# Retention in a hybrid decoder step: new tokens' outputs in four quarters of the array, scores in four banks, earlier copies of turned tokens

## The reference, cut to what matters

```
def retention_chunk(q, k, v, s_prev, log_gamma):
    scores = jnp.einsum('bihd,bjhd->bhij', qf, kf) * decay[None]
    o_intra = jnp.einsum('bhij,bjhe->bihe', scores, vf)
    q_decay = jnp.exp((idx + 1.0)[:, None] * log_gamma[None, :])
    o_inter = jnp.einsum('bihd,bhde->bihe', qf, s_prev) * q_decay[None, :, :, None]
    s_new = jnp.exp(C * log_gamma)[None, :, None, None] * s_prev + jnp.einsum('bjhd,hj,bjhe->bhde', kf, k_decay, vf)
    return o_intra + o_inter, s_new
```

## Time and profile before

| | |
|---|---|
| runs | 1435.70, 1435.81, 1437.54 us; median 1435.81 |
| profiled execution | 1436.48 us, of which the profile's span is 1434.7 us |
| busy in the span | PE 1374.4 us (96%), DVE 766.0 (53%), ACT 610.1 (43%), POOL 311.4 (22%) |
| mean granted clock of PE | 0.983 of full speed |

### The profile page before, as it was taken

The page is one execution under the profiler, slowest core; times in us unless marked ns, Lnnn a source line. Parts: engine busy times, 40 slices in busy tenths (PEclk is TensorE's granted clock), DMA queues, the critical chain, the costliest instruction groups (busy, mean ns, idle before and its releaser), DMA issues.

```text
span 1434.7 us, 31573 instructions
## 1 busy us (share of the span) xinstructions
PE 1374.4 (96%) x11123; PEld 1307.5 (91%) x11123; DVE 766.0 (53%) x1448; ACT 610.1 (43%) x1496; POOL 311.4 (22%) x487
## 2 busy tenths in 40 slices
PE   7984999999999999999989999999999999999998
PEld 7863888899999999999989888899999999999998
DVE  7772444536575575575554666455564443344443
ACT  3641333356565565565543444432233322233211
POOL 6530000046454555455410000000130000000000
PEclk9986999999999999999999999999999999999999
DMA  5123222166564565565545444332232222222232
GB/s 202 50 59 96 68 68 68 68 180 182 154 184 139 171 180 147 168 188 157 157 153 208 167 137 138 120 128 88 96 102 88 89 103 88 88 88 100 84 110 88
DMA packets 109325, 177.59 MB, mean 124 GB/s; under 512 B 13073, under 2 KB 84050, under 8 KB 107346
## 3 DMA queue, kind: packets, MB, share of 16 engines
q1 hardware_dynamic: 109202, 176.05, 38.4%
HBM read 163.98 MB, written 11.89 MB: 123 GB/s over the span
## 4 chain that ended last, share of the span: by engine, by line
PE 80%; DMA 4%; ACT 2%; DVE 2%; issue 2%; SPq 2%; POOL 0%; ACTq 0%; DVEq 0%; POOLq 0%
PE ps L1664 33%; PE ps L1376 24%; PE ps L1828 6%; PE ps L651 6%; PE ps L1402 2%; DMA z<-z_scratch 2%; PE ps L714 1%; PE ps L732 1%; PE ps L1882 1%; PE ps L1392 1%; DMA ring_raw<-in_wmain 1%; DMA ring_raw<-in_reto 1%; PE ps L724 1%; PE ps L1871 1%; SPq L983 0%
## 5 line engine op out<-in xcount | busy, mean ns | idle before, releaser
L1376 PE MATMUL ps<-wq_hi,ct_hi 128*128 128x260 f32 x1024 | 301.4, 294 | 1.4 <-POOL ct_lo L1052 1.4
L1376 PE MATMUL ps<-wq_hi,ct_lo 128*128 128x260 f32 x1024 | 289.5, 283 | 0.0
L1376 PE MATMUL ps<-wq_lo,ct_hi 128*128 128x260 f32 x1024 | 289.3, 283 | 0.0
L1052 POOL TENSOR_TENSOR ct_lo<-ct_raw,ct_hi 128x256 fp32r<-128x256 f32 x256 | 189.2, 739 | 390.4 <-ACT ct_hi L1111 196.8
L1220 DVE TENSOR_REDUCE k_sums<-k_squares 128x8 f32<-128x512 f32 (+1 forms) x256 | 175.3, 685 | 173.7 <-ACT k_squares L1118 171.4
L1118 ACT ACTIVATE k_squares<-ps 128x512 f32<-128x512 f32 x256 | 153.3, 599 | 164.4 <-PE ps L1376 160.3
L1376 PEld LDWEIGHTS ps<-wq_hi,ct_hi 128*128 128x128 f32 x1024 | 193.2, 189 | 4.9 <-issue 3.8
L1376 PEld LDWEIGHTS ps<-wq_lo,ct_hi 128*128 128x128 f32 x1024 | 193.1, 189 | 0.0
L1376 PEld LDWEIGHTS ps<-wq_hi,ct_lo 128*128 128x128 f32 x1024 | 192.6, 188 | 0.0
L1559 ACT ACTIVATE ring_hi<-ring_raw 128x1024 fp32r<-128x1024 f32 x88 | 89.1, 1013 | 167.6 <-PE ps L1664 120.4
L1564 DVE TENSOR_TENSOR ring_lo<-ring_raw,ring_hi 128x1024 fp32r<-128x1024 f32 x88 | 110.6, 1257 | 27.0 <-ACT ring_hi L1559 25.6
(11 more groups left out here) (324 smaller groups left out, 2967.1 us busy)
## 6 DMA issues: line engine op xcount, KB each, us to landing
ct_raw<-in_ct SPq DMA_DIRECT2D x256, 144.0 KB, 2.2
c_values<-in_c SPq DMA_DIRECT2D x256, 128.0 KB, 2.4
ring_raw<-in_wmain SPq DMA_DIRECT2D x40, 512.0 KB, 3.6
ring_raw<-in_up SPq DMA_DIRECT2D x32, 512.0 KB, 3.2
ring_raw<-in_down SPq DMA_DIRECT2D x32, 512.0 KB, 3.3
z_scratch<-z_staged SPq DMA_DIRECT2D x16, 268.0 KB, 2.2
z<-z_scratch SPq DMA_DIRECT2D x4, 1072.0 KB, 5.3
state_new<-in_state SPq DMA_DIRECT2D x4, 1024.0 KB, 4.8
```

Source lines behind the costliest of these rows:

```text
L1052: nc.gpsimd.tensor_tensor(ctl[:, j, :], ct[:, half, j, 0:KVL], cth[:, j, :].bitcast(F32), ALU.subtract).then_inc(ct_lo, 1)
L1376: mm = nc.tensor.matmul(k_ps[j % 2][:, f, 0:WQN], ch[:, j, r * P:(r + 1) * P], of_sequence(w, b)[:, r, f, :], start=(r == 0 and x == 0), s ...
```

## The change

- `new_outputs`: the masked queries get 32 columns each (24 of them zero), and product b goes to quarter b mod 4 of the array: rows 32 (b mod 4) and up of one PSUM bank. ACT copies the four partial tiles out together (`take_quarters`, r = 9), and at r = 10 PE adds them with one product with a constant 0/1 matrix (`sum_quarters`). Taking tile 5 out moves from r = 9 to r = 10.
- `scores`: tiles 2 and 3 go to the two banks of `ps[0]`, tile 4 to the first bank of `ps[1]`.
- ACT copies tiles 1, 3 and 5 of the turned tokens at the start of slots r = 3, 4, 5, ahead of the split.
- DVE runs `max_of_heads` in slot 2.
- The first mixing product waits for result tile k when it comes to it, not for all eight.

```
-                if slot == 3:
+                if slot == 2:
                     max_of_heads(b)
...
+    def score_place(self, t):
+        return self.ps[(1, 1, 0, 0, 1)[t]][:, t % 2, :]
...
             elif h:
                 pe.wait_ge(self.tok_out, self.copies * h)
+                pe.wait_ge(self.s_done, NT * h - 1)
+                pe.wait_ge(self.sm_done, NT * h - 1)
...
-            if t >= 2:
-                pe.wait_ge(self.sm_done, NT * h + t - 1)
-                pe.wait_ge(self.s_done, NT * h + t - 1)
+            if t in (2, 3):
+
+                pe.wait_ge(self.tok_out, self.copies * h + (2 * NT if t == 2 else self.copies))
+            if t == 4:
+                pe.wait_ge(self.sm_done, NT * h + 1)
+                pe.wait_ge(self.s_done, NT * h + 1)
...
             for b in range(NB):
-                mm = nc.tensor.matmul(ps[2][0:NB, NT % 2, 0:DV], self.qm[:, b, :], self.sd[:, b, :], start=(b == 0), stop=(b == NB - 1))
-            mm.then_inc(self.o_done, 1)
+                at = 32 * (b % 4)
+                mm = nc.tensor.matmul(ps[2][at:at + 32, NT % 2, 0:DV], self.qm[:, b, :], self.sd[:, b, :], start=(b < 4), stop=(b >= 4),
+                                      skip_group_check=True)
+            mm.then_inc(self.quad_done, 1)
+
+        def sum_quarters(h):
+            pe.wait_ge(self.quad_out, h + 1)
+            nc.tensor.matmul(ps[2][0:NB, NT % 2, 0:DV], m.const("sel"), self.quads[:], start=True, stop=True).then_inc(self.o_done, 1)
...
+                if r == 10:
+                    sum_quarters(h)
...
+        def take_quarters(h):
+            act.wait_ge(self.quad_done, h + 1)
+            nc.scalar.activation(self.quads[:], ps[2][:, NT % 2, 0:DV], ACT.Copy).then_inc(self.quad_out, 1)
...
         for slot in range(SLOTS + 1):
+            for h in range(RH):
+                r = slot - FIRST_HEAD - HEAD * h
+                if r in (3, 4, 5):
+                    tokens(h, 2 * r - 5)
             if slot % 2 == 0 and slot:
                 self.split_hi(act, slot // 2 + 1)
...
-                if r == 2:
-                    tokens(h, 0)
-                if r in (3, 4):
-                    tokens(h, 2 * r - 5)
+                if r in (2, 3, 4):
                     tokens(h, 2 * r - 4)
-                if r == 5:
-                    tokens(h, 5)
...
                 if r == 9:
+                    take_quarters(h)
+                if r == 10:
                     take(h, 5)
...
+        nc.vector.memset(self.qm[:], 0.0).then_inc(self.ss_set, 1)
...
-            pe.wait_ge(*((m.ret_lo, KD), (ot_lo, 1))[s])
+        if isinstance(i, int) and s:
+            pe.wait_ge(ot_lo, 1)
...
+                 ready=lambda pe, s, k: None if s else pe.wait_ge(m.ret_lo, k + 1),
```

More of the change, by code:

```diff
@@ L1726, in __init__ @@
         self.sm = p("scores_masked", [P, NT, P])
+        self.ss, self.uu, self.yy, self.tt = (p("o_" + x, [P, NT + 1]) for x in ("sums", "tmp2", "rms", "tmp"))
+        self.qm = p("q_masked", [P, NB, 32])
         self.vdt, self.junk = p("v_new_tok", [NB, DV]), p("sq_junk2", [P, DV])
-        self.qm = p("q_masked", [P, NB, NB])
-        self.ss, self.uu, self.yy, self.tt = (p("o_" + x, [P, NT + 1]) for x in ("sums", "tmp2", "rms", "tmp"))
+        self.quads = p("o_quarters", [P, DV])
         assert p.at <= m.small_end, (p.at, m.small_end)
@@ L1733, in __init__ @@
          self.refine, self.y_done, self.on_done, self.back, self.xr_done, self.xr_hi, self.xr_lo, self.st_out, self.sn_out,
-         self.ss_set, self.eps_done, self.half_done, self.half_out, self.sig_done, self.silu_done, self.gate_done, self.z_in, self.v_out, self.vb_in) = (sem("ret_" + x) for x in (
+         self.ss_set, self.eps_done, self.half_done, self.half_out, self.sig_done, self.silu_done, self.gate_done, self.z_in, self.v_out, self.vb_in, self.quad_done, self.quad_out) = (sem("ret_" + x) for x in (
              "rot_in", "sw_in", "rot_t", "rotated", "tok_turned", "qd_done", "tok_out", "sc_done", "sm_done", "u_done", "s_done",
              "o_done", "o_out", "sq_done", "sd_in", "masks", "grown", "snew", "chain", "y_done", "on_done", "back", "xr_done",
-             "xr_hi", "xr_lo", "st_out", "sn_out", "ss_set", "eps_done", "half_done", "half_out", "sig_done", "silu_done", "gate_done", "z_in", "v_out", "vb_in"))
+             "xr_hi", "xr_lo", "st_out", "sn_out", "ss_set", "eps_done", "half_done", "half_out", "sig_done", "silu_done", "gate_done", "z_in", "v_out", "vb_in", "quad_done", "quad_out"))
         self.rows = [min(P, NPROMPT - t * P) for t in range(NT)] + [NB]
@@ L1850, in scores @@
             n, t0 = rows[t], starts[t]
+            to = self.score_place(t)
             if t == 0:
@@ L1985, in result_hi @@
             nc.scalar.activation(m.rh(2 * h + e)[:, N_META:T], m.rl_raw(2 * h + e)[:, N_META:T], ACT.Copy).then_inc(self.xr_hi, 1)
-        act.wait_ge(self.ss_set, 2)
+        act.wait_ge(self.ss_set, 3)
         for slot in range(SLOTS + 1):
+            for h in range(RH):
+                r = slot - FIRST_HEAD - HEAD * h
+                if r in (3, 4, 5):
+                    tokens(h, 2 * r - 5)
             if slot % 2 == 0 and slot:
@@ L2059, in decays @@
             wait(dve, self.o_done, NO * h)
+            dve.wait_ge(self.ss_set, 3)
             nc.vector.tensor_tensor(self.qd[:, P:4 * P].rearrange("p (t i) -> p t i", i=P), self.qr[:, P:4 * P].rearrange("p (t i) -> p t i", i=P),
@@ L2069, in state @@
             dve.wait_ge(self.u_done, NT * h + t + 1)
-            nc.vector.tensor_tensor(self.sm[0:n, t, 0:n], ps[1][0:n, t % 2, 0:n], dmask[0:n, h, 0:n], ALU.mult).then_inc(self.sm_done, 1)
+            of = self.score_place(t)
+            nc.vector.tensor_tensor(self.sm[0:n, t, 0:n], of[0:n, 0:n], dmask[0:n, h, 0:n], ALU.mult).then_inc(self.sm_done, 1)
             if t == 0:
                 wait(dve, self.st_out, 16 * h)
-                nc.vector.tensor_copy(self.states[:, 0, :], ps[1][:, 0, P:P + DV]).then_inc(self.s_done, 1)
+                nc.vector.tensor_copy(self.states[:, 0, :], of[:, P:P + DV]).then_inc(self.s_done, 1)
             else:
@@ L2077, in state @@
                 nc.vector.scalar_tensor_tensor(self.states[:, t, :], self.states[:, t - 1, :], gamma[:, decay:decay + 1],
-                                               ps[1][:, t % 2, P:P + DV], ALU.mult, ALU.add).then_inc(self.s_done, 1)
+                                               of[:, P:P + DV], ALU.mult, ALU.add).then_inc(self.s_done, 1)
         def new_states(h, *samples):
```

7 lines of the change are left out of this document (3 added, 4 removed).

## The result

The changed kernel takes 1421.11 us (median of 4 runs, 1419.60 to 1422.04), the kernel before 1436.67 on the same chip (4 runs). The ratio is 0.9889, with a 95% interval of 0.9872 to 0.9906. The forecast was 1420.0, in a range of 1417 to 1426. The profiled execution of the changed kernel took 1422.04 us, of which the span is 1420.2; before it was 1436.48 and 1434.7.

A forecast was written before the change was run, and what follows sets the result against it. The prediction took the chain to stay on PE almost throughout, so time PE gets back counts. Its terms, -10.60 + 2.12 + 1.54 - 5.19 - 2.96 - 1.17 - 0.22 = -16.48, took 1436.48 us to 1420.0, range 1417 to 1426.

The forecast's parts named there:

- From product to turning back: New tokens' product up to the turning back, all four heads: quartered product, adding product and new waits taken together.
- quarters: New tokens' product: 16 instructions take 0.90 us instead of 3.55, four heads, -10.60 us.
- adding: Product summing the four partial tiles: 0.44 us plus 0.09 for stepping in, 0.53 a head, +2.12 us.
- new waits: PE waits for a `gates` row before slot r = 12, since tile 5 comes a slot later; +1.54 us.
- switching costs more: Rival: the adding product's switch in and out costs up to 0.38 us each side, 3.0 in all, 1423.0; chance 0.04.
- Turned tokens and the clock: Earlier copies remove 1.73 us before r = 3's second turn, heads 1 to 3 (-5.19); clock falls behind those waits vanish (-2.96).
- The new wait before r = 12: PE waits for DVE's `gates` row: 0.24 us in each of heads 0 to 2, 0.82 in head 3.
- The rival of the falling clock: Clock halves behind new waits or the mixing product's, 1.43 to 1.53 us each; 1421.5 to 1426; chance 0.25 including later chain.
- Scores: Tile 2 no longer waits for DVE to empty its bank: 0.39 us in heads 1 to 3, -1.17; nothing in head 0.
- The maxima: DVE's two steps a slot earlier: slot 4's gate starts at 741.45 instead of 741.67, -0.22 us.
- Nothing from single waits at the end: First mixing product: all eight result tiles are there when PE comes, so waiting for them singly gains nothing.
- the 2.0 us move along: Wait inside the mixing product hangs on a weight tile's load that follows the results, so it stays, 2.0 us.

The follow-up runs named there:

- one quarter for all: Changed kernel with all eight new-token products, 32 columns wide, sent to the first quarter of the array, copy and adding on 32 rows; 1430.58 us, ratio 0.9967.
- no quarters: Changed kernel with the new tokens' outputs as before: eight columns in one tile, no adding product; 1426.36 us, ratio 0.9935.
- Copies as before: Changed kernel with ACT copying the turned tokens in the old order, behind the split and the results' copies; 1430.07 us, ratio 0.9960.
- sum earlier: Changed kernel with the adding product moved to the middle of slot r = 10, behind the gate's second quarter; 1419.69 us, ratio 0.9888.
- loads apart: Changed kernel with SP's loads of heads 2 and 3 moved from slot 10 to slots 13 and 15; 1418.03 us, ratio 0.9881.
- maximum first: Changed kernel with DVE's two maximum steps at the end of slot 1, ahead of the split of slot 2's load; 1421.58 us, ratio 0.9904.

## Why the prediction was right, step by step

The forecast saving was 16.48 us, the profiled execution's 14.44. In B, where every step but the maxima lies, it was 16.26 against 15.70.

- *From product to turning back* (quarters -10.60, adding +2.12, new waits +1.54; sum -6.94): measured 45.11 - 51.23 = -6.12. The mechanism is right: "one quarter for all" shows that the quarters overlap, "no quarters" that they pay. The sizes were off by some 0.2 us a head. By head 1's rows: the product takes 1.00 and not 0.90; the slots on both sides of the adding product take 3.09 and 3.00 and not 2.94; the wait is 0.13 and not 0.24. What I had priced too low is the way out of a narrow product. From the earlier trace rows I took the 0.09 for stepping in; the kernel before also shows, behind the product that was there, a last row that takes 0.31 where the others take 0.22, and a first gate row that takes 0.23 where the next takes 0.12:

```profile
841.11 0.38 PE L1882 MATMUL ps<-state_new,q_masked 128*8 128x256 f32 x1
841.42 0.39 PE L1828 MATMUL ps<-x_hi,ring_hi 128*128 128x260 f32 x1
841.65 0.28 PE L1828 MATMUL ps<-x_lo,ring_hi 128*128 128x260 f32 x1
841.77 0.28 PE L1828 MATMUL ps<-x_hi,ring_lo 128*128 128x260 f32 x1
```

  The adding product pays all three, as head 3 shows in PE's timeline with the change:

```profile
915.84 0.28 PE L1834 MATMUL ps<-x_hi,ring_lo 128*128 128x260 f32 x1
916.05 0.60 PE L1901 MATMUL ps<-o_quarters,consts 128*8 128x256 f32 x2
916.58 0.39 PE L1834 MATMUL ps<-x_hi,ring_hi 128*128 128x260 f32 x1
916.80 0.28 PE L1834 MATMUL ps<-x_lo,ring_hi 128*128 128x260 f32 x1
916.92 0.29 PE L1834 MATMUL ps<-x_hi,ring_lo 128*128 128x260 f32 x1
```

  The gate row ahead of it takes 0.21, its two rows 0.53 instead of 2 x 0.22, the gate row behind it 0.22: 0.28 a head, of which I had counted 0.09. So the rival "switching costs more" came in part, with some 0.8 us of its 3.0. (The quarters' product keeps its own way out, hence 1.00 and not 0.90.) The Trainium skill (TensorEngine Tiling (Array Packing), Key Properties) has the engine emptied at a change of mode, not of the tile alone. The runs agree: the sixteen rows of the quarters start in four groups of four, 0.01 us apart within a group and 0.20 to 0.22 from one group to the next, so four instructions go through in the time that one took before. The first group of head 1, merged (the second starts at 833.50):

```profile
833.26 0.42 PE L1895 MATMUL ps<-state_new,q_masked 128*32 128x256 f32 x4
```

- *Turned tokens and the clock* (-5.19 - 2.96 = -8.15): measured -8.20. "Copies as before" brings back the waits and the two falls of the clock. It also shows that the two terms are not independent of the quarters: with quarters the old order would cost 9.6. The sum was right because I took the copies' gain against the old kernel and let the quarters' gain stand in full behind it.
- *The new wait before r = 12* (0.24 and 0.82): measured 0.12 to 0.14 and 0.78, by "sum earlier". The chain that I read off head 1 is the one that sets it. The rival of the falling clock did not come: the clock is 1.00 behind these waits in both executions of the changed kernel. Behind the wait inside the mixing product, which the rival also named, it came in one of ten traces (last section).
- *Scores* (-1.17, nothing in head 0): measured -1.36. Tile 2 comes 0.38 sooner, and the rest of the 0.46 a head I did not trace. For head 0 the reason was right, and "loads apart" shows it.
- *The maxima* (-0.22): slot 4's first row starts 2.17 behind the end of ACT's copy (742.16 - 738.93 - 1.06), where it was 2.40 by the earlier trace rows: -0.23. The wait in front of line 1415 is no measure of it: it fell from 1.80 to 0.65, but was 1.66 when the changed kernel ran again. It follows the load. So A's -0.80 is 0.23 of the change and otherwise the luck of slot 2's load and of the spread; run again, A was 0.60 longer than before.
- *Nothing from single waits at the end; the 2.0 us move along*: from turning back to the mixing product it took 7.42 and takes 7.40. The wait of 2.0 reads 2.5 here, but 2.0 again in "maximum first", which has the whole change; its cause lies in the queue of loads.
- The 1.5 us that the profiled execution lost ahead of the slots are scatter: the run again has 727.30 there.

## What to carry to other kernels

A masked product with few columns that is repeated into one small tile is worth spreading over the array's quarters, if the adding product and what its later result holds up are counted with it: here 10.3 us gross, 6.1 net. When two edits shorten the ways into one meeting point (PE and ACT at the turns), each alone is worth less than its part of both together (4.7 + 8.2 of 14.3, with the scores' 1.4 taken off each). A wait that "stays" deserves a look at what is queued ahead of its releaser: the two that stayed here were transfers behind larger loads in the same queue, and freeing them, with the sum moved half a slot, gave 7.3 us more on top of the change's 15.6.

## What the runs showed of the hardware that I had not expected

Whether the clock falls is not a matter of a wait's length alone, nor of its place. The wait inside the mixing product, 2.0 to 2.7 us long, is in ten of the thirteen traces, and the clock fell behind one of them. Behind that one, a wait of 2.37 us in "no quarters", and behind the one of 2.52 in the changed kernel, the windows of PE read, in this order:

```profile
946.11:950.00 3.89, 3.89 (x20) 0.57 0.45 137
```

```profile
942.04:946.00 3.96, 3.96 (x33) 1.00 0.41 133
```

The first ran mostly at the lower of the two levels, 1.2 GHz, and got 20 instructions done where the other did 33; its stretch C is 1.4 us longer. The wait in front of the row that spreads the maximum is in eleven traces, 0.6 to 1.8 us long. It was hit once, in "copies as before", where it lasted 1.36; the 1.66 of the changed kernel run again were spared:

```profile
739.92:743.92 4.00, 3.96 (x22) 0.67 0.51 168
```

```profile
740.86:744.86 4.00, 3.96 (x32) 1.00 0.54 162
```

The waits before the turns behaved the same in both kernels that had them: the first and third cost clock, the second none. The Trainium skill (TensorE: Matmul & The Clock Gate, Part 1) says that the monitor behind the clock runs on its own time; the runs agree so far as the longer of two waits at one place was spared both times. Why the same two of three are hit in two kernels, four of six waits there against two of twenty-one at the other two places, stays open.
